# One-hot gate weights scaled on ScalarE instead of VectorE, with the hand-over into the expert loop reordered

## The reference, cut to what matters

```python
q = (xb @ w_query).reshape(T, PEER_HEADS, 2, PEER_DKEY // 2)
s = jnp.einsum('thpd,phkd->thpk', q, sub_keys).astype(jnp.float32)
sv_, si = lax.top_k(s, PEER_TOPK)
cand = ...        # sums of the two halves' scores, 256 for each head
top_s, pos = lax.top_k(cand, PEER_TOPK)
idx = jnp.take_along_axis(cand_idx, pos, axis=-1)
g = jax.nn.softmax(top_s, axis=-1)
u = expert_u[idx]
act = jax.nn.gelu(jnp.einsum('td,thkd->thk', xb, u).astype(jnp.float32))
return jnp.einsum('thk,thkd->td', (g * act).astype(xb.dtype), expert_v[idx])
```

## Time and profile before

| | us |
|---|---|
| runs: lowest, median, highest of 3 | 2033.68, 2039.81, 2040.74 |
| the profiled execution | 2033.83 |
| its span, first to last instruction | 2032.0 |
| PE busy | 1905.5 (94%) |
| DVE busy | 1365.7 (67%) |
| ACT busy | 767.8 (38%) |
| POOL busy | 451.5 (22%) |

### The profile page before, as it was taken

One profiled execution on the slowest core, in us unless ns is written; L12 is line 12 of the kernel. 1 busy time (PEld: TensorE's weight loads), 2 busy tenths in 40 slices (PEclk: granted clock), 3 DMA queues, 4 the chain that ended last, 5 costly groups with the idle time before them and its releaser, 6 DMA issues.

```text
span 2032.0 us, 28421 instructions
## 1 busy us (share of the span) xinstructions
PE 1905.5 (94%) x11158; PEld 1719.1 (85%) x11158; DVE 1365.7 (67%) x2416; ACT 767.8 (38%) x1046; POOL 451.5 (22%) x377
## 2 busy tenths in 40 slices
PE   7999988897979999998999699998999999999996
PEld 2799965697979999998999699998888888888875
DVE  4433364535268986889877997886367777777776
ACT  1222254412115455454455254553443333333332
POOL 0111100001101462334622354335301111111000
PEclk9999999888999999999999899998999999999998
DMA  7534231032115898988988799999967878777642
GB/s 286 199 139 153 96 132 52 1 104 81 45 32 163 293 352 285 314 285 305 372 289 288 256 329 331 314 317 386 352 243 254 317 255 310 262 302 270 247 179 94
DMA packets 187608, 471.65 MB, mean 232 GB/s; under 512 B 11900, under 2 KB 79064, under 8 KB 183256
## 3 DMA queue, kind: packets, MB, share of 16 engines
q1 hardware_dynamic: 141400, 302.11, 42.5%
q0 software_dynamic: 46080, 167.79, 23.0%
HBM read 414.54 MB, written 55.31 MB: 231 GB/s over the span
## 4 chain that ended last, share of the span: by engine, by line
PE 82%; DVE 10%; DMA 4%; ACT 2%; issue 1%; POOL 0%; SPq 0%; DVEq 0%; ACTq 0%
PE PS L988 25%; PE PS L539 12%; PE PS L541 12%; PE PS L540 12%; PE PS L901 4%; PE PS L935 4%; PE PS L909 2%; DVE gat L1744 2%; DMA gat<-in_peer_u_dram,idx 1%; PE PS L564 1%; DMA uraw<-in_peer_u_dram 1%; DMA G<-gates_dram 1%; PE PS L602 1%; PE PS L847 1%; PE PS L574 1%
## 5 line engine op out<-in xcount | busy, mean ns | idle before, releaser
L539 PE MATMUL PS<-XH,uth 128*128 128x384 f32 x1024 | 359.4, 351 | 0.0
L540 PE MATMUL PS<-XL,uth 128*128 128x384 f32 x1024 | 347.2, 339 | 0.0
L541 PE MATMUL PS<-XH,utl 128*128 128x384 f32 x1024 | 346.3, 338 | 0.0
L1403 POOL DMA_INDIRECT gat<-in_peer_v_dram,idx x160 | 189.2, 1183 | 556.0 <-DVE acc L1765 499.5
L1403 POOL DMA_INDIRECT gat<-in_peer_u_dram,idx x160 | 202.6, 1266 | 366.1 <-DVE a L1744 295.1
L1878 DVE TENSOR_TENSOR vl<-vrw,vh 128x1024 fp32r<-128x1024 f32 x128 | 156.8, 1225 | 147.9 <-ACT vh L1291 147.9
L1291 ACT ACTIVATE vh<-vrw 128x1024 fp32r<-128x1024 f32 x128 | 135.6, 1060 | 314.6 <-PE PS L988 303.0
L988 PE MATMUL PS<-vh,wh 128*128 128x512 f32 x768 | 242.8, 398 | 5.4 <-DVE wl L1880 2.8
L539 PE MATMUL PS<-XH,whi 128*128 128x272 f32 x784 | 230.9, 295 | 14.9 <-DVE XL L1685 8.2
L988 PE MATMUL PS<-vh,wl 128*128 128x512 f32 x768 | 240.7, 394 | 0.0
L988 PE MATMUL PS<-vl,wh 128*128 128x512 f32 x768 | 239.2, 393 | 0.0
(11 more groups left out here) (284 smaller groups left out, 3193.4 us busy)
## 6 DMA issues: line engine op xcount, KB each, us to landing
uraw<-in_peer_u_dram SPq DMA_DIRECT2D x128, 512.0 KB
vrw<-in_peer_v_dram SPq DMA_DIRECT2D x64, 1024.0 KB, 5.0
acts_dram<-gel SPq DMA_DIRECT2D x128, 192.0 KB
gates_dram<-gst SPq DMA_DIRECT2D x24, 1024.0 KB
al<-acts_dram SPq DMA_DIRECT2D x16, 1536.0 KB, 8.7
G<-gates_dram SPq DMA_DIRECT2D x16, 1536.0 KB, 13.2
adaw<-in_w_ada_dram SPq DMA_DIRECT2D x8, 2048.0 KB, 8.0
wraw<-in_w_in_dram SPq DMA_DIRECT2D x7, 2048.0 KB, 7.9
```

Of the source, the lines that this page charges most:

```text
L539: mm(out, ah, bh, start=start, stop=False)
L540: mm(out, ah, bl, start=False, stop=False)
L541: return mm(out, al, bh, start=False, stop=stop)
L1403: nc.gpsimd.indirect_dma_start(out=gat[:, n % NGAT, :], out_offset=None, in_=table, in_offset=bass.IndirectOffsetOnAxis(ap=idx[:, k:k + 1] ...
```

## The change

It has four parts. (1) `one_hot` on DVE loses its multiplication and builds `ohA` first; ACT gets `scale_hot`, which multiplies each of the four tokens' rows by its column of `selT` in an activation of 128x128, in place, eight in a gate step, between `u_lo` and `gelu`. (2) `rep` is formed before `first_level(0)`, `turn(0)` goes between the last scores on PE, and `u_hi(0)` goes ahead of the last score copy on ACT. (3) The last two entries of `EXP_AT` and `GELU_AT` become later steps. (4) An unused semaphore is dropped.

```diff
-EXP_AT = (2, 6, 20, 54, 86)
+EXP_AT = (2, 6, 20, 56, 87)
-GELU_AT = 80
+GELU_AT = 84
...
+        pe.wait_ge(gemms[2].ev, CREDIT + 15)
+        turn(0)
+        score(0, 14)
         pe.wait_ge(gemms[2].ev, CREDIT + 16)
-        score(0, 14)
         score(0, 15)
...
         token_major(2, 0)
-        turn(0)
         scores_sample()
...
+        def scale_hot(i, g):
+            gi = NG * (i - 2) + g
+            act.wait_ge(s_hot, gi + 1)
+            for x in range(OG):
+                row = ohB[:, gi % 2, x, :]
+                last = act_(row, row, ACT.Copy, scale=selT[:, 2, OG * g + x:OG * g + x + 1])
+            last.then_inc(s_oh, 1)
...
+        u_hi(0)
         scores_out(0, 3)
         token_major(0, x3, 2)
-        u_hi(0)
...
+            for i in range(2, 5):
+                first = GATE_PER[i] * (m - GATE_AT[i])
+                if 0 <= first < NG:
+                    for g in range(first, min(NG, first + GATE_PER[i])):
+                        scale_hot(i, g)
             gelu(m)
...
+                dve.wait_ge(norms[1].lo, 2 * KD)
+                tt(rep[:, 0], f(XH[:, :, TP - P:TP]), f(XL[:, :, TP - P:TP]), ALU.add).then_inc(s_rep, 1)
...
                 first_level(0)
...
-                tt(ohB[:, sl], line, bc(selT[:, 0, cols], 2, P), ALU.is_equal).then_inc(s_cch, 1)
...
                 tt(ohA[:, sl], line, bc(selT[:, 1, cols], 2, P), ALU.is_equal)
+                tt(ohB[:, sl], line, bc(selT[:, 0, cols], 2, P), ALU.is_equal).then_inc(s_hot, 1)
                 fill(FILL_HOT[i])
-                dve.wait_ge(s_cch, upto)
-                tt(ohB[:, sl], ohB[:, sl], bc(selT[:, 2, cols], 2, P), ALU.mult).then_inc(s_oh, 1)
```

More of the change, by code:

```diff
@@ L318, in build @@
         st = Stage()
-        st.sq, st.ss, st.sd, st.rs, st.tmp, st.y, st.hi, st.lo = (
-            sem(f"s_n{n}_{x}") for x in ("sq", "ss", "sd", "rs", "tmp", "y", "hi", "lo"))
+        st.sq, st.ss, st.sd, st.tmp, st.y, st.hi, st.lo = (
+            sem(f"s_n{n}_{x}") for x in ("sq", "ss", "sd", "tmp", "y", "hi", "lo"))
         norms.append(st)
@@ L348, in build @@
     s_selT, s_selTe = sem("s_selT"), sem("s_selTe")
+    s_hot = sem("s_hot")
     s_oh, s_gmm, s_gev = sem("s_oh"), sem("s_gmm"), sem("s_gev")
@@ L595, in gemm_chunk, with turn @@
             last.then_inc(st.mm, 1)
+        def turn(m):
+            pe.wait_ge(s_u[m % 2], 16 * (m // 2) + 16)
+            if m >= 1:
+                pe.wait_ge(s_utl, m)
+            for k in range(KD):
+                last = mm(PS[:, k // 4, (k % 4) * P:(k % 4 + 1) * P], uraw[:, m % 2, k * P:(k + 1) * P], ident,
+                          start=(k % 4 == 0), stop=(k % 4 == 3), is_transpose=True, skip_group_check=True)
+            last.then_inc(s_ut, 1)
         def score(i, hp):
@@ L893, in token_major @@
             last.then_inc(s_xt, 1)
[L895 to L903, removed]
         def less_hi(m):
@@ L1452, in gemm_lo @@
             if st is gemms[2]:
+                dve.wait_ge(norms[1].lo, 2 * KD)
+                tt(rep[:, 0], f(XH[:, :, TP - P:TP]), f(XL[:, :, TP - P:TP]), ALU.add).then_inc(s_rep, 1)
+                tt(rep[:, 1].rearrange("p k (q t) -> p k q t", q=4), bc(f(XH[:, :, TP:T]), 2, 4),
+                   bc(f(XL[:, :, TP:T]), 2, 4), ALU.add).then_inc(s_rep, 1)
                 first_level(0)
@@ L1720, in _ @@
         first_level(3)
-        tt(rep[:, 0], f(XH[:, :, TP - P:TP]), f(XL[:, :, TP - P:TP]), ALU.add).then_inc(s_rep, 1)
-        tt(rep[:, 1].rearrange("p k (q t) -> p k q t", q=4), bc(f(XH[:, :, TP:T]), 2, 4), bc(f(XL[:, :, TP:T]), 2, 4),
-           ALU.add).then_inc(s_rep, 1)
         tt(sum4[:], ident[:, 0:TS], ident[:, TS:2 * TS], ALU.add).then_inc(s_dch, 1)
@@ L1846, in one_hot @@
                 line = bc(iota, 1, OG)
-                tt(ohB[:, sl], line, bc(selT[:, 0, cols], 2, P), ALU.is_equal).then_inc(s_cch, 1)
-                steps[0] += 1
-                upto = steps[0]
                 tt(ohA[:, sl], line, bc(selT[:, 1, cols], 2, P), ALU.is_equal)
+                tt(ohB[:, sl], line, bc(selT[:, 0, cols], 2, P), ALU.is_equal).then_inc(s_hot, 1)
                 fill(FILL_HOT[i])
-                dve.wait_ge(s_cch, upto)
-                tt(ohB[:, sl], ohB[:, sl], bc(selT[:, 2, cols], 2, P), ALU.mult).then_inc(s_oh, 1)
         choose(0)
```

## The result

The changed kernel takes 2062.81 us in the median of four runs (2056.99 to 2065.79), the kernel before 2038.13 us in the median of four runs on the same chip (2033.68 to 2040.74). The ratio is 1.0132, with a 95% interval of 1.0114 to 1.0151: slower by 1.3%, 27 us. The forecast was 2064 us.

What follows compares the result with a forecast made beforehand. PE was taken to bound the gates, DVE's `choose` (or nearly) the stretches in tiles 3 and 4. Terms 32.1 - 7.2 + 0.2 + 2.1 = +27.2 us gave 2061 to 2067, stated as 2064; range 2042 to 2085.

Steps and rivals of the forecast that it cites:

- 48 gate steps: Gates of tiles 2 to 4: PE waits for the scaling, a step grows from 7.34 to 8.05 us, +32.1 us.
- hand-over, net of step 6: Second `turn` 9.4 us earlier, partly lost at step 6 where ACT waits for `choose(1)`; -7.2 us remains.
- tile 3, step 46 to 63: ACT's 6.57 us wait becomes some 8 us of PE at `sel_turn(3)`; -1.2 and 1.4 for slower clock, +0.2 us.
- tile 4, step 80 to 96: The 19.61 us GELU wait moves elsewhere; `sel_turn(4)` 1.3 us later, 0.8 for slower clock, +2.1 us.
- Engine time: Gates: four tokens cost DVE 0.686 us, ACT 1.17; +46 us, of which ACT's gaps hide part, hence +32.1.
- What `choose(2)` has to spare at `sel_turn(2)`: Tile 2: DVE has seconds to spare there, so PE keeps the hand-over's 7.2 us.
- my 1.4: Tile 3: PE's half clock behind its wait, before inside DVE's time, now behind it, priced at 1.4 us.
- a small term: Tile 4: DVE waits 3.5 us for the later GELU, so `sel_turn(4)` comes at 1248.0 instead of 1246.72, +1.3 us.
- The 0.8 for a slower clock behind `sel_turn(4)`: Tile 4: PE's slower clock behind its wait there, priced at 0.8 us, half of the figure for tile 3.
- A: Gates: activations follow every 0.20 us or less, so the scaling hides; +3.7 in place of +32.1, 2036 us; chance 0.13.
- B: Waits in tiles 3 and 4 do go away, DVE finishing `choose` some 20 us sooner; 2035 us; chance 0.05.
- C: Gates: activations do not overlap, or PE's clock is lower in steps with waits; +63, 2100 us; chance 0.06.

Runs made afterwards that it cites:

- the split kernel: Changed kernel with each step's first group of four scaling activations moved ahead of `u_lo`, the second left ahead of `gelu`: 2027.0 us, ratio 0.9952.
- part 2 alone: The kernel before with only the new hand-over (`rep`, `turn(0)` and `u_hi(0)` moved): 2029.04 us, ratio 0.9968.
- the scaling alone: The kernel before with only the weight multiplication moved from DVE to ACT, between `u_lo` and the GELU: 2063.47 us, ratio 1.0153.

## Why the prediction was right, and where its sizes were off

The sum on the profiled execution was +27.2 us and +23.2 came. The terms, with what the table of GELU starts and the rows show:

| term | forecast, us | the same by the steps named here, us | measured, us |
|---|---|---|---|
| 48 gate steps | +32.1 | +34.1 | +37.4 |
| hand-over, net of step 6 | -7.2 | -7.2 | -7.6 |
| earlier already ahead of the hand-over | 0 | 0 | -1.9 |
| tile 3, step 46 to 63 | +0.2 | -0.8 | +2.2 |
| tile 4, step 80 to 96 | +2.1 | +1.1 | -0.6 |
| step 114 to the end | 0 | 0 | -6.3 |

The third column is there because the forecast counts otherwise than the steps do. It puts the last two gate steps of tile 2, and of tile 3, at 0.44 us together and leaves the other 0.98 us of each pair to the stretch behind. Every one of the 48 steps lost 0.78 us at its own place, so here all 48 stand at the forecast's 0.71, and the two stretches are 0.98 less.

**The gate steps: mechanism right, each step 0.07 us too small.** One activation takes 388 ns (389 forecast), eight take 2.43 us as forecast. The Trainium skill, ScalarE: Activation LUTs, section What ACT_TABLE_LOAD costs, puts a pointer operand at about 93 ns; the 91 ns above agree. The first wait is 0.42 us (858.61 less the 858.19 at which PE, with its matmuls of a half step 0.175 apart, would have begun the gates), near the 0.44 forecast. The second group starts on PE 1.17 us behind the first, as 1.17 us of activations would have it: 0.28 more than the 0.89 of a group, beside 0.27 forecast. Behind it, though, PE needs 0.97 us to the next `turn`, not 0.89 (851.66 to 852.63). PE's timeline, in windows that part the first product of a group from its other seven:

```profile
850.49 0.35 PE L938 MATMUL PS<-ohB,ohA 128*128 128x128 f32 x1 [0.26 <-ACT ohB L1276]
850.68 0.94 PE L938 MATMUL PS<-ohB,ohA 128*128 128x128 f32 x7
851.66 0.35 PE L938 MATMUL PS<-ohB,ohA 128*128 128x128 f32 x1
851.85 0.94 PE L938 MATMUL PS<-ohB,ohA 128*128 128x128 f32 x7
```

Behind a wait the second product begins 0.19 us after the first, where the products of a group otherwise follow every 0.11 us. These 0.08 us come behind both waits. Behind the first they vanish in the wait for the second group; behind the second they lengthen the step. The forecast had no term for them: 48 x 0.08 is 3.8 us, less 0.5 for the waits.

The Trainium skill, ScalarE: Activation LUTs, section Rules for kernel authors, puts multiplications on VectorE; the result has the sign of that rule. Engine time, by which the prediction turned the rule into +46 us, did not decide: the split kernel has the same activations on ACT (121.7 us in all, 116.6 here) and no loss.

**The hand-over: right.** The second `turn` on PE is at 597.04, 11.49 us earlier than in the earlier trace rows. PE's timeline there:

```profile
587.35 0.38 PE L613 MATMUL PS<-skT,qT 128*128 128x128 f32 x2
587.57 1.04 PE L604 MATMUL PS<-cst,uraw 128*128 128x128 f32 x8
...
593.88 1.04 PE L905 MATMUL PS<-cst,rep 128*128 128x128 f32 x8
...
597.04 1.06 PE L604 MATMUL PS<-cst,uraw 128*128 128x128 f32 x8 [1.66 <-ACT utl L1253]
```

The scores in which `turn(0)` now stands began 1.94 us earlier than before already (587.35 against 589.29 there), so the change made 9.55 of it, forecast 9.4. The granted clock, before 0.50 from 595.3 to 602, in and behind the wait for `rep`, is 1.00 there now. At step 6 1.95 us were lost again, forecast 2.1; ACT waited 2.70 us for the score buffer there, forecast 3.1. What `choose(2)` has to spare at `sel_turn(2)` is not seconds, as the prediction says, but at most some 11 us: its `sel` is written at 764.27 before and PE turns it at 775.10, after at 754.05 and 765.56.

**Tile 3: right place, two prices wrong.** The wait moved as the prediction said. PE's timeline, `sel_turn(3)` and the `turn` behind it:

```profile
1010.64 0.90 PE L947 MATMUL PS<-cst,sel 128*128 128x128 f32 x3 [9.64 <-DVEq L1852]
1011.34 1.91 PE L604 MATMUL PS<-cst,uraw 128*128 128x128 f32 x8
```

The exponential's wait of 6.57 us is gone and 9.64 us stand here, forecast 8. The slower clock behind it (0.50 granted from 1010.6 to 1016.4, before 1.00 behind `sel_turn(3)`) cost more than my 1.4: from `sel_turn` to the GELU of step 63 it is 8.86 us, and before it was 1014.37 - 1008.22 = 6.15, so 2.7. And DVE was slower: counted from step 46, `sel_turn(3)` came 0.5 us earlier, where the forecast (1.2 and the 0.98 above) makes 2.2. From its first search to `sel_turn`, `choose(3)` took 109.05 us, before 107.29; in it DVE waited 8.6 us for gathered rows, before 6.2.

**Tile 4: right mechanism, sign of a small term wrong.** ACT no longer waits at the GELU of the gathered products, DVE does, on its timeline:

```profile
1182.58 0.29 DVE L1790 TENSOR_TENSOR a<-a,g 128x128 f32<-128x128 f32 x1 [5.15 <-ACT a L1292]
```

5.15 us, forecast 3.5: the GELU came where forecast, 22.6 us behind that of step 80, and DVE was there 1.6 us sooner than I had it, which fits the last two multiplications of tile 3's gates (2 x 0.686 us): they went from ahead of `choose(4)` too, and I had counted such a pair ahead of `choose(3)` only. PE stands at the exponential of step 87 and at `sel_turn(4)`:

```profile
1216.62 1.22 PE L912 MATMUL PS<-uth,negI 128*128 128x512 f32 x2 [15.15 <-ACT uth L1249]
...
1263.71 0.55 PE L947 MATMUL PS<-cst,sel 128*128 128x128 f32 x3 [3.24 <-DVEq L1852]
```

Forecast were some 17 for the first, and no figure for the second. Counted from step 80, `sel_turn(4)` came 0.6 us sooner, where the forecast (1248.0 less 1143.0) has it 0.3 later. DVE needed 81.1 us from the GELU's result to `sel_turn`. Before it needed 82.1, from 1162.42 to 1244.5, where its last row began; PE came there only at 1246.72 and did not wait. Waits for gathered rows make 0.7 of this 1.0 (8.1 us before, 7.4 after); the rest was not traced. The 0.8 for a slower clock behind `sel_turn(4)` did not come (6.15 us from there to the GELU of step 96, before 6.08).

**The tail: a term I had at nothing.** Near step 115 PE waits for the DMA of a block of `expert_u`: 5.2 us, before 8.5. In the other kernels this wait is 5.0 to 8.6 us, 5.0 with part 2 alone (gate steps of 7.34 us) and 7.3 with the scaling alone (8.12), so the length of a gate step does not set it. The granted clock from step 114 to 127 is 0.96, before 0.94. From the last GELU to the end of the span it is 565.9 us after and 568.0 before, and 565.5 to 570.6 in the seven experiments that leave that part alone. The difference begins at its start, where PE waits for DVE ahead of the first `down`: 1.3 us after, and the clock stays at 1.00; 2.6 us before, and it is 0.50 from 1465.7 to 1468.9. The wait is 1.0 to 1.3 us in all four kernels with 565.5 to 565.9 us, and 1.8 to 3.4 in the five with 568.0 or more. One of the four multiplies nothing and has gate steps of 7.34 us, the other three have 8.12. With one profile of each kernel, whether the change has a part in these 6.3 us stays open.

The four terms that belong to the change come to +31.4 us, 4.2 more than summed. The profiled execution was also 8.2 us shorter ahead of the hand-over and behind step 114, and no run shows that the change did that. So the mechanism came as forecast, and that the time came out within 2 us is partly luck. By its median the change costs 24.7 us, by its ratio 27 (23 to 31); the sum said 27.2.

The rivals: A, that the scaling hides, failed for the reason given against it, the pointer's 91 ns; with a constant scale it is nearly true. It is wholly true in another place in ACT's order, which the prediction did not ask about. B fell with the old steps put back. Nothing of C came: the eight activations overlap (2.43 us, not 3.11), and the clock in steps with waits is 1.00 with 113.01 us busy of 118.

## What to carry to other kernels

Work moved to an engine with idle time is free only if it fits into the gap at its own place in that engine's order: eight activations of 2.43 us cost 0.78 us a step behind `u_lo`, where PE waited for them next, and nothing with four of them ahead of it, so read the receiving engine's gaps one by one and cut the work to them. Moving a waiting instruction to a later step moves no work, and the 20 us of waits only changed their line. What took them away was moving work of the engine that bounds the stretch into one where it waits itself (137.8 us of DVE's waits in the gates): the ratio went from 0.9952 to 0.9833.

## What the runs showed of the hardware that I had not expected

A wait of PE ahead of a group of small matmuls cost 0.08 us more than the wait itself: behind it the second product began 0.19 us after the first (851.66 and 851.85), where the others follow every 0.11 us, and eight took 0.97 us to the next `turn` where they take 1.78 / 2 = 0.89 without a wait. In the gates PE kept its full clock, 1.00, although each step of 8.12 us holds two waits of less than half a us, while behind the one wait of 9.64 us it was 0.50, the 1.2 GHz level, and eight transposes took 1.91 us, where they take 1.04 in a gate step. And the same scaling of 128x128 follows its neighbour every 0.29 us with its scale in a column of `selT` ((2.43 - 0.39) / 7), and every 0.20 us with a constant ((1.70 - 0.30) / 7, with the 301 ns of the earlier trace rows for the last).
